# Moving one late conditioning unit ahead of the logits, and both picks ahead of a copy, in a two-layer diffusion step

## The reference

```
def trunk_layer(x, c_vec, lp, ctx_cache, pos):
    shift1, scale1, gate1, shift2, scale2, gate2 = adaln(c_vec, lp['w_ada'], lp['b_ada'])
    h = rms_norm(x, lp['norm1']) * (1 + scale1) + shift1
    ...                                     # conv branch and attention branch, merged
    x = x + gate1 * ((g_conv * conv_out + g_att * att) @ lp['w_out'])
    h2 = rms_norm(x, lp['norm2']) * (1 + scale2) + shift2
    x = x + gate2 * hier_moe(h2, ...)

def adaln(c_vec, w_ada, b_ada):
    mod = silu(c_vec) @ w_ada + b_ada       # 1024 x 6144, for two conditioning vectors
    return split(mod, 6)

def hier_moe(h, ...):
    # 4 groups of 4 experts: the best group by its logits, in it the best two experts,
    # SwiGLU of width 256, weighted sum
```

## Time and profile before

| | us |
|---|---|
| median of 3 runs | 974.01 |
| lowest, highest | 973.48, 977.22 |
| the profiled execution, its own time | 979.21 |
| its span, first to last instruction | 977.4 |
| PE busy | 927.7 (95%) |
| DVE busy | 726.9 (74%) |
| ACT busy | 501.2 (51%) |
| DMA | 206.75 MB, mean 212 GB/s |

### The profile page before, as it was taken

One profiled execution on the slowest core, in us unless ns is written; L12 is line 12 of the kernel. 1 busy time (PEld: TensorE's weight loads), 2 busy tenths in 40 slices (PEclk: granted clock), 3 DMA queues, 4 the chain that ended last, 5 costly groups with the idle time before them and its releaser, 6 DMA issues.

```text
span 977.4 us, 15475 instructions
## 1 busy us (share of the span) xinstructions
PE 927.7 (95%) x5998; PEld 770.9 (79%) x5998; DVE 726.9 (74%) x1214; ACT 501.2 (51%) x718; POOL 39.6 (4%) x62
## 2 busy tenths in 40 slices
PE   3999999989999999999999999998899999999997
PEld 2797789767888778887778968996589977888776
DVE  3568799474855689869956697995658568986995
ACT  4243623375422478647754445226663247874772
POOL 1000000032000000000010000001400000000000
PEclk9899999999999799999999999999999999999999
DMA  9953456501655679939939324541123258993971
GB/s 372 369 213 131 168 223 230 201 1 45 231 199 216 254 291 362 361 129 346 385 128 384 113 109 172 232 157 44 44 93 130 81 192 325 361 372 127 326 277 65
DMA packets 29019, 206.75 MB, mean 212 GB/s; under 512 B 3408, under 2 KB 3440, under 8 KB 4240
## 3 DMA queue, kind: packets, MB, share of 16 engines
q1 hardware_dynamic: 28656, 204.81, 55.5%
q0 software_dynamic: 288, 0.92, 0.3%
HBM read 203.98 MB, written 1.74 MB: 210 GB/s over the span
## 4 chain that ended last, share of the span: by engine, by line
PE 80%; DVE 10%; ACT 5%; issue 3%; DMA 1%; DVEq 0%; SPq 0%; ACTq 0%
PE ps L866 57%; PE ps L853 6%; PE ps L877 4%; PE ps L844 2%; PE ps L1331 2%; DVE w_lo L733 2%; PE ps L1154 1%; PE ps L1071 1%; DVE w_lo L728 1%; ACT w_hi L722 1%; DVE x L2359 1%; ACT kT L1611 1%; DMA x<-x 1%; PE ps L1142 1%; PE ps L1426 1%
## 5 line engine op out<-in xcount | busy, mean ns | idle before, releaser
L733 DVE TENSOR_TENSOR w_lo<-ring,w_hi 128x2048 fp32r<-128x2048 f32 (+2 forms) x102 | 225.8, 2222 | 21.6 <-ACT w_hi L1717 20.8
L866 PE MATMUL ps<-h_hi,w_hi 128*128 128x384 f32 x576 | 198.1, 344 | 6.3 <-issue 2.4
L1717 ACT ACTIVATE w_hi<-ring 128x2048 fp32r<-128x2048 f32 x96 | 183.1, 1914 | 20.8 <-PE ps L866 20.8
L866 PE MATMUL ps<-h_hi,w_lo 128*128 128x384 f32 x576 | 193.4, 336 | 0.0
L866 PE MATMUL ps<-h_lo,w_hi 128*128 128x384 f32 x576 | 193.3, 336 | 0.0
L866 PEld LDWEIGHTS ps<-h_hi,w_hi 128*128 128x128 f32 x576 | 108.1, 188 | 20.8 <-issue 13.0
L728 DVE TENSOR_TENSOR w_lo<-ring,w_hi 128x2048 fp32r<-128x2048 f32 x41 | 93.7, 2289 | 33.3 <-ACT w_hi L722 33.3
L866 PEld LDWEIGHTS ps<-h_lo,w_hi 128*128 128x128 f32 x576 | 108.2, 188 | 0.0
L866 PEld LDWEIGHTS ps<-h_hi,w_lo 128*128 128x128 f32 x576 | 108.1, 188 | 0.0
L1961 DVE SCALAR_TENSOR_TENSOR z<-u,par,z 128x399 f32<-128x399 f32 x180 | 104.7, 632 | 1.5
L866 PE MATMUL ps<-w_hi,hg_hi 128*128 128x512 f32 x256 | 103.2, 403 | 0.8 <-DVE hg_lo L733 0.8
(11 more groups left out here) (270 smaller groups left out, 1407.7 us busy)
## 6 DMA issues: line engine op xcount, KB each, us to landing
ring<-wpre SPq DMA_DIRECT2D x96, 1024.0 KB, 6.9
ring<-wmoe SPq DMA_DIRECT2D x96, 1024.0 KB, 6.5
x<-x SPq DMA_DIRECT2D x1, 1536.0 KB, 7.6
x_out<-x SPq DMA_DIRECT2D x4, 384.0 KB, 3.2
par<-par_in POOLq DMA_DIRECT2D x2, 367.5 KB, 7.0
const<-const_in SPq DMA_DIRECT2D x1, 314.0 KB, 3.1
ckv_out<-ckvT POOLq DMA_DIRECT2D x2, 64.0 KB, 5.1
kr_out<-kr POOLq DMA_DIRECT2D x2, 16.0 KB, 5.1
```

Source lines behind the costliest of these rows:

```text
L733: return nc.vector.tensor_tensor(out, whole, leading.bitcast(F32), ALU.subtract)
L866: m = mm(out, a, b, start=(start and i == 0 and j == 0), stop=(stop and i == n - 1 and j == 2))
L1717: af(w_hi[m % MOE_PLACES], slot(moe_slot(l, m)), ACT.Copy).then_inc(split_hi, 1)
```

## The change

Late unit 1 is issued directly behind late unit 0, ahead of the logits, instead of between the transposes and the rank. PE's wait for `adaT_taken` moves from ahead of the loop to ahead of the first `gather_weights`, behind the first expert's up product. On DVE the pick of group 1 comes ahead of `ada_copy`.

```
-                ada(rest[0])
+                for e in rest[:2]:
+                    ada(e)
                 fold_rows()
...
                 for c in range(HROW_EARLY, KD):
                     turn_rows(c)
-                ada(rest[1])
                 out = begin("rank")
                 pe.wait_ge(onehot_ready, l + 1)
...
                 wait_taken(pe, l, "rank")
                 wait_taken(pe, l, "srow")
-                pe.wait_ge(adaT_taken, batches_before(l, "late") + 1)
                 settle(pe)
...
                         pe.wait_ge(cw_ready, pe.snap(i + PAIRS))
+
+                        pe.wait_ge(adaT_taken, batches_before(l, "late") + 1)
                         gather_weights(i)
...
-                make_pick(0, lambda: ada_copy(batches_before(l, "late") + 1))
+                make_pick(0)
+                ada_copy(batches_before(l, "late") + 1)
                 dve.wait_ge(routed, l + 1)
```

## The result

| | before | changed |
|---|---|---|
| median, us | 974.31 (6 runs) | 979.47 (6 runs) |
| lowest, highest | 973.48, 977.22 | 977.35, 981.45 |
| ratio of the runs, 95% interval | | 1.0049, 1.0028 to 1.0070 |
| the profiled execution, its own time (span) | 979.21 (977.4) | 981.45 (979.7) |
| mean granted clock of the profiled execution | 0.985 | 0.982 |

The change costs some 4.8 us, 2.7 to 6.8 (the ratio is one of means; the medians are 5.2 apart). I had forecast 974.7 and a range up to 978.0, so the size was wrong and the measured time lies above the range. The two profiled executions are only 2.2 us apart. That difference is itself part of the answer.

A forecast was written before the change was run, and what follows sets the result against it. PE was taken to bound the first layer up to the first expert product, DVE's queue the second. Terms of -0.8 and +1.5 us net +0.7, moving the median from 974.01 to 974.7; range 972.2 to 978.0.

The forecast's parts named there:

- The base: Both layers read from one profiled execution of 979.21 us: first layer bound by PE, second by DVE around the copy.
- Gain 0.8: First layer: rank starts at 324.8 instead of 325.58, so copy and first expert product come 0.8 us earlier.
- Part 1, the clock term: Small matmuls behind the moved unit, ahead of the rank, run at half clock: 0.2 us, from zero to 0.87.
- Part 1, the later routing: Logits to transposes and DVE's routing 1.07 us later; second layer's L2233 and first pick 0.64 later, first layer's queue not binding.
- Part 2, the second pick: DVE's second pick ahead of the copy: price zero in the first layer, 0.85 us in the second.
- queue terms: DVE's second layer: routing 0.64 us later plus second pick 0.85, moving the copy by 1.49.
- the sign that I had named for being wrong: Second layer: a copy that waits for PE, instead of starting at the end of the sixth pick operation.
- Part 3: Wait for `adaT_taken` moved behind the up product: zero gain, bounds nothing and 0.2 us, as PE's pass-count load ends later.
- Part 4: Ring slots of late units 0 and 1 free sooner, two expert units land earlier: price zero.
- (b): Rival, clearly slower: low clock lasts through units 2, 3 and gather to 804.3; 5 us more, 979.7; chance 0.03.
- The rule of the Trainium skill: Rival, slower by the clock: PE idle around second layer's `ada_columns` brings half clock; +0.8 to +1.7, near 976.0; chance 0.25.
- The range: Whole kernel: cases' 971.6 to 976.7, said to be widened above by the three runs' spread: 972.2 to 978.0.

The follow-up runs named there:

- g4: Kernel before with late unit 1 behind the rank, together with units 2 and 3; median 981.04 against 974.77, ratio 1.0056.
- h1: g4 plus eight dummy matmuls (constant operand, result never read) between transposes and rank; median 976.29 against 974.46 before, ratio 1.0030.
- g1: The changed kernel measured again, all parts, no further edit; median 978.96 against 974.77 before, ratio 1.0043.
- e3: Changed kernel plus eight dummy matmuls between transposes and rank, where late unit 1 stood before; median 978.51 against 974.70 before, ratio 1.0036.
- e4: Kernel before run once more without any edit, as a control; median 975.68 against 974.70, ratio 1.0008.
- e2: Kernel before with only the pick order changed, both picks ahead of the copy; median 978.60 against 974.70, ratio 1.0035.
- f6: e2 plus eight dummy matmuls between late unit 3 and `ada_columns`; median 978.26 against 974.71 before, ratio 1.0026.
- g3: Kernel before with only the wait for `adaT_taken` moved behind the first up product; median 975.21 against 974.77, ratio 1.0004.
- f7: Kernel before plus six dummy matmuls ahead of `ada_columns`; median 974.72 against 974.71, ratio 0.9994.

## Why the prediction was wrong

- **The base (failed).** I took the first layer of one execution, at 979.21, for the rule, and wrote myself that it stood 5.2 us above the median. Its long low stretch ahead of the rank is not the rule there: of the eight traces that keep unit 1 right before the rank, five have none in the first layer. "Gain 0.8" for the first layer holds in such an execution (measured: 0.2, at the start of the product); in the others that layer is like the second, and the loss is there too. With +1.5 for both layers my own terms would have given +3.0, which lies in the measured interval.
- **Part 1, the clock term (failed).** I priced the clock only by the work pushed past the moment at which it falls, 0.2 us, and held its stretches fixed. The unit between transposes and rank was work that kept the clock up. With it moved behind the rank, nothing added ahead of the logits and the pick order as before (g4), the kernel loses 5.5 us; dummy work in its place gives back about half of that by the means, 70% by the medians (h1). In the changed kernel the clock's median fell from 0.992 to 0.986 (g1), and late units 2 and 3 ran at half clock in both layers.
- **Part 1, the later routing (right in the second layer, wrong in the first).** In the second layer the rank gains nothing (7.8 us behind late unit 0 in g1, 7.9 in the profiled kernel before, at low clock) and L2234 follows the `hrow_lo` at once, as I had said; against late unit 0 it came 0.4 later, not 0.64, since the clock term of 0.2 ahead of the rank did not show. In the first layer I let the transposes end last; in the changed kernel they ran at full clock and PE waited 1.58 us for `oh_r`. At full clock the rank comes 0.87 later (e3 against e4), and with it all of DVE's routing.
- **Part 2, the second pick (half right).** At full clock the copy moved as worked out (e3: product +1.5 for both queue terms; e2 and f6: 0.7 for the pick, where I had 0.85). I had zero for the first layer, which is right only with a low clock. In the profiled changed kernel the copy of the second layer waited for PE, the sign that I had named for being wrong. The low stretch over the gather in e2's second layer need not be the pick's doing: e4 and g3 have one in their first layer without it, and f6, with PE's idle time there filled, has one in both.
- **Part 3 (right).** g3: 1.0004, and 0.9990 to 1.0018. The sequencer's rows said it before.
- **Part 4 (right as far as seen).** No trace shows a wait for expert weights there.
- **The rivals.** (b), with a chance of 0.03, is what the profiled execution of the changed kernel did in the second layer: low from 790.6 to 804.0, for which I had written up to 804.3. Its price, 979.7, is 0.2 from the measured median, and that is luck: a usual execution reaches it with shorter stretches in both layers, and a us at half clock costs less than the 0.5 us in that price. The rule of the Trainium skill (TensorE: Matmul & The Clock Gate, section Why this matters for your kernels), that idle gaps bring the clock back to half, named the right side. The traces agree with it only in part: in g4 the clock fell at 320.3, and PE had been busy for all 6.20 us from 316.00 to 322.20, with matmuls of 1 to 20 columns from 317.1 to 320.2; the idle time (PE busy for 0.10 of 0.80 us) came within the low stretch.
- **The range (failed).** The cases' own figures were 971.6 to 976.7. The 978.0 does not follow from them: widened by the spread of the three runs before, as the text says, the upper end would have been 980.4, and the measured time inside it.

What stays open: how the 4.8 us divide between clock and queue in a given run, and so which of the two failed steps weighs more. They cover each other (at low clock the picks are hidden, at full clock they show), so only the ends are known: 3.0 us of queue terms with the clock kept (the products of e3; +3.5 in its time), and 5.5 us with some 0.9 of queue terms (g4). The changed kernel with the clock given back (e3) is not measurably faster than without. Why the clock falls in one execution and not in the next of the same kernel is open too.

## What to carry to other kernels

A unit of work in a sparse stretch may be what keeps TensorE's clock up; before moving it, read the granted clock behind the stretch in several executions, and price the following matmuls at both levels. Compare the profiled execution's time and mean clock with the median of the runs first: if it is in the tail, its long stretches are not the usual ones. Two costs that hide each other, here a slow PE and a longer DVE queue, are not to be added; work out which ends last at either clock.

## What the runs showed that I had not expected

Adding eight matmuls per layer whose result nobody reads made a kernel faster, by 3.0 us by the means and more by the medians (g4 to h1). And an extra us at half clock costs only 0.32 us of span in the kernel before, not 0.5. A likely reason is that part of the low time lies where DVE is the bound: 3.4 us of low clock over the gather moved the product only from 19.67 to 19.87 (first layers of f7 and g3).
